# Samples' convolution taps as one GpSimd product and one VectorE sum, prompt taps in two chains, fewer taps on TensorE

## What is computed

```
def causal_dwconv(h, buf, w, b):          # h (B,T,C), buf (B,K-1,C), w (K,C), b (C)
    full = jnp.concatenate([buf.astype(h.dtype), h], axis=1)
    out = lax.conv_general_dilated(full, w[:, None, :], window_strides=(1,), padding="VALID", ...)
    return out + b.astype(h.dtype), full[:, full.shape[1] - (k - 1):]
...
proj = h @ p["w_in_ab"][i]
ya, pb = multi_scale_pool(xa, pool_bufs[i], start_pos, ...)
glu = a * jax.nn.sigmoid(gt)
c, cb = causal_dwconv(glu, conv_bufs[i], p["conv_w"][i], p["conv_b"][i])
yb = jax.nn.silu(layernorm(c, ...))
x = x + jnp.concatenate([ya, yb], axis=-1) @ p["w_out_ab"][i]
```

## Time and profile before

| | |
|---|---|
| median of 3 runs | 1206.99 us (1206.85 to 1207.07) |
| profiled execution | 1207.7 us, of which the traced span is 1205.9 us |
| PE, matmuls busy | 1186.9 us, 98% of the span |
| DVE / ACT / POOL busy | 741.7 / 508.6 / 623.7 us |
| stretch of units 3 to 11 and the convolution | from about 29 to 133 us of the span |

### The profile page before, as it was taken

How to read it: one execution, slowest core, us unless ns; L and a number is a source line. 1 busy time by engine, 2 the same in 40 slices (tenths; PEclk the granted TensorE clock), 3 DMA queues, 4 the chain that set the end, 5 groups by cost and what they waited for, 6 DMA issues and landing times.

```text
span 1205.9 us, 21702 instructions
## 1 busy us (share of the span) xinstructions
PE 1186.9 (98%) x8636; PEld 1156.7 (96%) x8636; DVE 741.7 (62%) x1499; ACT 508.6 (42%) x880; POOL 623.7 (52%) x632
## 2 busy tenths in 40 slices
PE   7999999999999999999999999999999999999997
PEld 7887799999999999999999999999999999999997
DVE  5999555567945688454521754345687557865554
ACT  6333455445434454343521532344443344433442
POOL 4643435436963469543455323443489344884433
PEclk9999999999999999999999999999999999999999
DMA  6310124321332213422322221322214222242212
GB/s 241 112 36 27 44 67 139 105 70 35 106 140 70 70 35 106 141 74 67 123 88 82 64 84 62 122 71 88 70 36 157 88 70 70 70 141 71 66 54 79
DMA packets 33652, 103.74 MB, mean 86 GB/s; under 512 B 4880, under 2 KB 6928, under 8 KB 33552
## 3 DMA queue, kind: packets, MB, share of 16 engines
q1 hardware_dynamic: 29488, 98.92, 25.0%
q10 hardware_dynamic: 4080, 3.69, 1.0%
HBM read 98.29 MB, written 4.79 MB: 85 GB/s over the span
## 4 chain that ended last, share of the span: by engine, by line
PE 89%; DVE 4%; ACT 2%; DMA 1%; issue 1%; POOL 1%; ACTq 0%; POOLq 0%; SPq 0%; DVEq 0%
PE psum L408 67%; PE psum L606 13%; PE psum L504 3%; PE psum L736 3%; DVE psum L1846 1%; DVE psum L1734 1%; PE psum L448 1%; POOL w_lo L1340 1%; DVE squares_sum L2002 1%; DMA w_raw<-in_w_down 1%; PE psum L686 1%; DVE block_lo L1734 1%; PE psum L456 0%; ACT psum L1061 0%; DVE arena L1971 0%
## 5 line engine op out<-in xcount | busy, mean ns | idle before, releaser
L408 PE MATMUL psum<-x_hi,w_hi 128*128 128x288 f32 x1856 | 402.0, 298 | 6.7 <-ACT w_hi L782 6.7
L408 PE MATMUL psum<-x_hi,w_lo 128*128 128x288 f32 x1856 | 398.6, 296 | 1.1 <-POOL w_lo L1260 1.1
L408 PE MATMUL psum<-x_lo,w_hi 128*128 128x288 f32 x1856 | 398.2, 296 | 0.0
L1260 POOL TENSOR_TENSOR w_lo<-w_raw,w_hi 128x1024 fp32r<-128x1024 f32 (+2 forms) x102 | 226.8, 2228 | 275.3 <-ACT w_hi L782 275.3
L408 PEld LDWEIGHTS psum<-x_hi,w_hi 128*128 128x128 f32 x1856 | 300.0, 189 | 8.8 <-ACT w_hi L782 6.6
L408 PEld LDWEIGHTS psum<-x_hi,w_lo 128*128 128x128 f32 x1856 | 299.9, 189 | 1.5 <-POOL w_lo L1260 1.5
L408 PEld LDWEIGHTS psum<-x_lo,w_hi 128*128 128x128 f32 x1856 | 300.0, 189 | 0.0
L1846 DVE SCALAR_TENSOR_TENSOR psum<-arena,params,psum 128x608 f32<-128x608 f32 x176 | 150.6, 856 | 88.5 <-ACT psum L1061 84.1
L1260 POOL TENSOR_TENSOR w_lo<-arena,w_hi 128x1024 fp32r<-128x1024 f32 (+1 forms) x49 | 114.6, 2338 | 119.9 <-ACT w_hi L782 119.9
L782 ACT ACTIVATE w_hi<-w_raw 128x1024 fp32r<-128x1024 f32 (+2 forms) x102 | 98.5, 970 | 88.5 <-PE psum L408 79.6
L606 PE MATMUL psum<-block_hi,w_hi 128*128 128x288 f32 x448 | 133.4, 298 | 0.2 <-POOL w_lo L1340 0.2
(11 more groups left out here) (208 smaller groups left out, 1619.2 us busy)
## 6 DMA issues: line engine op xcount, KB each, us to landing
w_raw<-in_w_up SPq DMA_DIRECT2D x44, 512.0 KB, 3.4
arena<-in_w_up SPq DMA_DIRECT2D x44, 512.0 KB, 3.4
w_raw<-in_w_down SPq DMA_DIRECT2D x16, 512.0 KB, 3.6
arena<-in_w_down SPq DMA_DIRECT2D x16, 512.0 KB, 3.6
w_raw<-in_w_in_c SPq DMA_DIRECT2D x16, 512.0 KB, 3.3
w_raw<-in_w_in_ab SPq DMA_DIRECT2D x12, 512.0 KB, 3.6
w_raw<-in_w_out_ab SPq DMA_DIRECT2D x16, 256.0 KB, 2.6
w_raw<-in_w_out_c SPq DMA_DIRECT2D x8, 512.0 KB, 3.4
```

Source lines behind the costliest of these rows:

```text
L408: last = nc.tensor.matmul(PS[:, 2 * (q % 2 if slot is None else slot) + half, 0:HALF], w[q][:, k * P:(k + 1) * P], r[:, r_at, half * HALF: ...
L1260: nc.gpsimd.tensor_tensor(w_lo[slot][:, 0:nk * P], raws[RAW_SLOT[RAW[u]]][:, 0:nk * P], w_hi[slot][:, 0:nk * P].bitcast(F32), ALU.subtract ...
```

## The change

The taps that PE does for the prompt are 6, 7, 7 and 10 for the four groups, and so DVE's are 25, 24, 24 and 21. DVE does them in two chains by even and odd taps, in the banks S1 and M1, and a new function `merge(c)` adds the two. For the samples POOL multiplies in one instruction (`sample_products`) each of 64 outputs' 31 inputs by the 31 tap weights, 1984 products for each partition, into a buffer `tap_products`; DVE sums over the taps with one `tensor_reduce` (`sum_samples`) and adds the bias with one `tensor_scalar` in `merge`. `sample_products(c)` for c > 0 waits until DVE has summed the group before, since there is one buffer. The chains "s" and "r" and `combine_samples` are gone.

```diff
-    PE_TAPS = 10
-    V_TAPS = TAPS - PE_TAPS
+    PE_TAPS = (6, 7, 7, 10)
+    V_TAPS = [TAPS - n for n in PE_TAPS]
...
-        tap_w = cut(XA0 + KH * XL + KH * GL, PE_TAPS, P)
+        tap_w = cut(XA0 + KH * XL + KH * GL, max(PE_TAPS), P)
+        tap_products = mem[:, (KD + KH) * T:(KD + KH) * T + SM * TAPS].rearrange("p (s t k) -> p s t k", s=NS, t=DS)
...
-                for n in range(PE_TAPS):
-                    k = V_TAPS + n
-                    pe.wait_ge(tap_w_ready, PE_TAPS * c + n + 1)
+                for n in range(PE_TAPS[c]):
+                    k = V_TAPS[c] + n
+                    pe.wait_ge(tap_w_ready, sum(PE_TAPS[:c]) + n + 1)
                     last = nc.tensor.matmul(PS[:, S0, 0:PR], tap_w[:, n, :], glu[:, c, k:k + PR],
-                                            start=(n == 0), stop=(n == PE_TAPS - 1))
+                                            start=(n == 0), stop=(n == PE_TAPS[c] - 1))
                 last.then_inc(conv_mm, 1)
...
-                for n in range(PE_TAPS):
+                for n in range(PE_TAPS[c]):
                     nc.scalar.activation(tap_w[:, n, :], ident[:, :], ACT.Copy,
-                                         scale=pcol("conv_w", (TAPS - PE_TAPS + n) * KH + c)).then_inc(tap_w_ready, 1)
+                                         scale=pcol("conv_w", (V_TAPS[c] + n) * KH + c)).then_inc(tap_w_ready, 1)
...
+            def sample_products(c):
+
+                pool.wait_ge(glu_ready, 2 * c + 2)
+                if c:
+                    pool.wait_ge(taps_summed, c)
+                else:
+                    pool.wait_ge(ld_par, 16)
+                first = glu[:, c, CB + PR:CB + PR + 1]
+                weights = pcol("conv_w", c)
+                nc.gpsimd.tensor_tensor(tap_products,
+                                        bass.AP(first.tensor, first.offset, [first.ap[0], [CB + DS, NS], [1, DS], [1, TAPS]]),
+                                        bass.AP(weights.tensor, weights.offset, [weights.ap[0], [0, NS], [0, DS], [KH, TAPS]]),
+                                        ALU.mult).then_inc(tap_products_ready, 1)
+
             for u in range(1, N_IN0):
                 split_n(u + 3)
+                if u in (2, 5, 8, 11):
+                    sample_products(u // 3)
                 if u in (3, 6, 9):
                     windows(u // 3 - 1)
...
-            steps_made = [0]
-
             def conv(c, first, end):
 
                 dve.wait_ge(glu_ready, 2 * c + 2)
-                if first == 0:
-                    behind.update(p=0, s=0, r=0)
-
-                def step(chain, out, k, acc, win, last=False):
-                    w = pcol("conv_w", k * KH + c)
-                    if behind[chain]:
-                        dve.wait_ge(conv_step, behind[chain])
-                        ins = nc.vector.scalar_tensor_tensor(out=out if last else acc, in0=win, scalar=w, in1=acc,
-                                                             op0=ALU.mult, op1=ALU.add)
-                    elif chain == "r":
+                if c and first == 0:
+                    dve.wait_ge(taps_merged, c)
+                for k in range(first, end):
+                    acc, win, w = PS[:, (S1, M1)[k % 2], 0:PR], glu[:, c, k:k + PR], pcol("conv_w", k * KH + c)
+                    if k == 0:
+                        ins = nc.vector.tensor_scalar(acc, win, w, pcol("conv_b", c), ALU.mult, ALU.add)
+                    elif k == 1:
                         ins = nc.vector.tensor_scalar(acc, win, w, None, ALU.mult)
                     else:
-                        ins = nc.vector.tensor_scalar(acc, win, w, pcol("conv_b", c), ALU.mult, ALU.add)
+                        dve.wait_ge(conv_step, sum(V_TAPS[:c]) + k - 1)
+                        ins = nc.vector.scalar_tensor_tensor(out=conv_o[:, c, 0:PR] if k == V_TAPS[c] - 1 else acc,
+                                                             in0=win, scalar=w, in1=acc, op0=ALU.mult, op1=ALU.add)
                     ins.then_inc(conv_step, 1)
-                    steps_made[0] += 1
-                    behind[chain] = steps_made[0]
-
-                new = smp(conv_o[:, c, PR:T])
-                samples = lambda k: smp(glu[:, c, CB + PR:GL], CB + DS)[:, :, k:k + DS]
-                for k in range(first, end):
-                    last = k == V_TAPS - 1
-                    step("p", conv_o[:, c, 0:PR], k, PS[:, S1, 0:PR], glu[:, c, k:k + PR], last)
-                    step("s", new, k, smp(PS[:, M1, 0:SM]), samples(k), last)
-                    if k % 2:
-                        step("r", None, V_TAPS + k // 2, smp(PS[:, M1, SM:2 * SM]), samples(V_TAPS + k // 2))
-
-            behind = dict(p=0, s=0, r=0)
-            CONV_STEPS = V_TAPS + TAPS
-            assert V_TAPS // 2 == PE_TAPS
+
+            def sum_samples(c):
+                dve.wait_ge(tap_products_ready, c + 1)
+                nc.vector.tensor_reduce(smp(conv_o[:, c, PR:T]), tap_products, AX.X, ALU.add).then_inc(taps_summed, 1)
+
+            def merge(c):
+
+                dve.wait_ge(conv_step, sum(V_TAPS[:c + 1]))
+                nc.vector.tensor_tensor(conv_o[:, c, 0:PR], PS[:, (S1, M1)[V_TAPS[c] % 2], 0:PR], conv_o[:, c, 0:PR],
+                                        ALU.add).then_inc(taps_merged, 1)
+                dve.wait_ge(taps_summed, c + 1)
+                nc.vector.tensor_scalar(conv_o[:, c, PR:T], conv_o[:, c, PR:T], pcol("conv_b", c), None, ALU.add)\
+                    .then_inc(conv_samples, 1)
 
             def combine(c):
 
                 dve.wait_ge(conv_mm, c + 1)
-                dve.wait_ge(conv_step, CONV_STEPS * (c + 1))
+                dve.wait_ge(taps_merged, c + 1)
                 nc.vector.tensor_tensor(conv_o[:, c, 0:PR], PS[:, S0, 0:PR], conv_o[:, c, 0:PR], ALU.add)\
                     .then_inc(conv_whole, 1)
-
-            def combine_samples(c):
-                dve.wait_ge(conv_step, CONV_STEPS * (c + 1))
-                nc.vector.tensor_tensor(conv_o[:, c, PR:T], PS[:, M1, SM:2 * SM], conv_o[:, c, PR:T], ALU.add)\
-                    .then_inc(conv_samples, 1)
...
@@ -1609,39 +1618,42 @@
             make_glu(0)
             conv(0, 0, 7)
             evacuate(3)
-            conv(0, 7, 14)
+            conv(0, 7, 15)
             evacuate(4)
-            conv(0, 14, V_TAPS)
             make_glu(1)
-            combine_samples(0)
-            conv(1, 0, 5)
+            conv(0, 15, V_TAPS[0])
+            sum_samples(0)
+            merge(0)
+            conv(1, 0, 2)
             combine(0)
-            conv(1, 5, 8)
             evacuate(5)
-            conv(1, 8, 14)
+            conv(1, 2, 10)
             evacuate(6)
-            conv(1, 14, 19)
+            conv(1, 10, 18)
             evacuate(7)
-            conv(1, 19, V_TAPS)
             make_glu(2)
-            combine_samples(1)
-            conv(2, 0, 5)
+            conv(1, 18, V_TAPS[1])
+            sum_samples(1)
+            merge(1)
+            conv(2, 0, 4)
             combine(1)
-            conv(2, 5, 9)
+            conv(2, 4, 6)
             evacuate(8)
-            conv(2, 9, 15)
+            conv(2, 6, 13)
             evacuate(9)
-            conv(2, 15, 20)
+            conv(2, 13, 20)
             evacuate(10)
-            conv(2, 20, V_TAPS)
             make_glu(3)
-            combine_samples(2)
-            conv(3, 0, 9)
+            conv(2, 20, V_TAPS[2])
+            sum_samples(2)
+            merge(2)
+            conv(3, 0, 3)
             combine(2)
-            conv(3, 9, 15)
+            conv(3, 3, 8)
             evacuate(11)
-            conv(3, 15, V_TAPS)
-            combine_samples(3)
+            conv(3, 8, V_TAPS[3])
+            sum_samples(3)
+            merge(3)
             combine(3)
```

More of the change, by code:

```diff
@@ L29 @@
 ACT = mybir.ActivationFunctionType
+AX = mybir.AxisListType
 P = 128
@@ L299, in hybrid_trunk @@
         conv_samples = sem("conv_samples")
+        tap_products_ready, taps_summed, taps_merged = sem("tap_products_ready"), sem("taps_summed"), sem("taps_merged")
         new_packed = sem("new_packed")
```

## The result

| | before | after |
|---|---|---|
| median of 6 runs each, us | 1207.19 (1206.85 to 1207.80) | 1212.54 (1211.11 to 1215.63) |
| profiled execution, time and span, us | 1207.7, 1205.9 | 1212.39, 1210.7 |
| start of `conv_mean` | 133.09 | 135.96 |
| length of `conv_mean` | 3.88 | 5.81 |

The ratio is 1.0046, with an interval of 1.0036 to 1.0056: slower by 0.46%. 1210.7 us was forecast, within 1204 to 1215.

What follows compares the result with a forecast made beforehand. PE was taken to bound the kernel, with DVE nearly as full. PE's saved 8.6 us would be lost to DVE's stalls of 13.35 and 3.3 us, `conv_mean` starting 3.7 us late: 1210.7 us, range 1204 to 1215.

Steps and rivals of the forecast that it cites:

- PE's part: Ten taps leave PE, 8.64 us; if nobody is late, `conv_mean` starts at 124.45 instead of 133.09.
- The forecast's 12 us of PE waiting for DVE: PE waits about 12 us for DVE, in pieces over units 7 and 10, the last taps and `conv_mean`.
- DVE's plain work: DVE's steps, merges, biases and sums without stalls: 24.1 us gone, 18.1 new, net 6.0 us less.
- POOL's product: Length T of POOL's one multiplication of 1984 columns: 4.9 us, between 3.6 and 5.5.
- rival C: A longer POOL product because weights are read four columns apart: 1212.5 us, or near 1215 or 1218; chance 0.15.
- The stalls at the bias: DVE's bias of groups 0, 1 and 2 waits for POOL's just-begun product: three times 4.45, 13.35 us.
- Rival A: No stall at DVE's bias, since so short or in-place an instruction passes POOL: 1198.4 us; chance 0.17.
- rival B: Fewer or shorter bias stalls: product 3.6 us, or POOL still at a low part for group 0; 1206.8 or 1206.2; chance 0.20.
- The glus: DVE's glus of groups 1 and 2 meet POOL's work: 2.7 and 0.6 us, together 3.3, between 0 and 6.
- The sum: All DVE terms added: `conv_mean` starts at 136.8 instead of 133.09, 3.7 us late.
- the branch of the forecast that had 0.48: Main case: POOL's product of 4.4 to 5.4 us, three bias stalls, 1209.2 to 1212.2 us; chance 0.48.
- Rival D, PE's clock: PE's clock restarting slower after gaps of a few us: hidden while PE waits for DVE, given nothing; no chance stated.

Runs made afterwards that it cites:

- first experiment: The changed kernel, but POOL's product of the next group waits for the bias of the group before instead of its sum; 1198.88 us, ratio 0.9935.
- The packed weights: The changed kernel, but ACT first copies each group's 31 tap weights side by side and POOL's product reads them there; 1210.14 us, ratio 1.0025.

## Why the prediction was right or wrong

**What bounds, and PE's part.** Right. PE's list got 8.6 us shorter, and `conv_mean` could have started near 124.5: with the stalls gone it starts at 124.64 (first experiment). The forecast's 12 us of PE waiting for DVE are there as 4.57 + 1.46 + 2.81 us of waits (for the 1.46 the view names no releaser; the wait ends at 119.03, 0.1 us behind DVE's combine of group 2, which these taps wait for) and some 2.4 us of matmuls at the lower clock between 93.9 and 99.4, whose pairs start 0.48 us apart there and 0.27 behind; together 11.2.

**DVE's plain work.** Right within 0.9 us. The sum takes 2.21 us where 2.13 and its end were taken from the additions, the tap steps keep 0.66 (eight from 60.34 on take 5.35 us, half of it beside POOL's product, eight from 66.27 on 5.34), and two chains cost nothing. DVE's last combine began at 135.18; less the stalls of 16.3 us that is 118.9, of which 0.37 is the wait for PE; the forecast had 119.4 without waits.

**POOL's product.** Mis-sized: T is 5.56 us, not 4.9, and just over the upper end of 5.5. I took the ns a column of the multiplications with few columns; 1984 columns go at (5.56 - 0.19) / 1984 = 2.71 ns, close to the slowest row. The packed weights, at 2.02 ns, show that a quarter of it is how the weights lie. The rule that rival C takes from the Trainium skill, "GPSIMD Engine Reference", section "Performance pitfalls for Q7 kernels" (half more cycles for a read step over 8 bytes), has the direction; on 4.19 us it would make 6.2, an estimate, and 5.56 was measured.

**The stalls at the bias.** The mechanism was right: the bias, 64 columns and in place, does wait, for the whole of POOL's instruction under way. Rival A fell. Two stalls of 4.98 us were there and not three of 4.45; the third escaped through rival B's mechanism (POOL still at its low parts), by 0.3 us, while the forecast had POOL free "by 1 us". POOL was free at 57.55, near the 57.1 of the forecast, but DVE's sum was over at 56.65 and not at 58.4, mostly because group 1's glu had lost 1.2 us and not 2.7. Group 3's bias, forecast to meet none, met a low part and lost 0.83. With 0.18 at group 0 that is 10.97 us in all against 13.35.

**The glus.** Mis-sized the other way: 5.3 us against 3.3. The one of group 2 was given 0.6 us and lost 3.5, for each of its two instructions waited for a low part of 2.4 us. Group 1's lost 1.2 where 2.7 were set, and group 3's, set at nothing, 0.6. The forecast's range for the glus, 0 to 6, held it.

**The sum.** 136.8 was forecast for `conv_mean`, 135.96 came: -0.5 of plain work and DVE's one wait, -2.4 of biases, +2.0 of glus. Part of the agreement is luck: errors of 2.4 and 2.0 us cancel. The 1212.54 us stand just above the branch of the forecast that had 0.48 (three stalls, 1209.2 to 1212.2) and on rival C's 1212.5, but C's three stalls of 5.05 us were not there: two stalls and the clock made the number, and its agreement with C is chance.

**Rival D, PE's clock.** This is the step that failed. "A slower restart would be hidden: behind the last taps PE has some 6 us until DVE is ready. I give it nothing." It is hidden after the gap before 93.93, as said. But the last gap stands directly ahead of `conv_mean`, where nothing of DVE's lateness is left to hide behind, and there it cost 1.93 us. Of these 1.7 are the clock, since `conv_mean` takes 4.12 us at full clock behind a wait (first experiment), and 0.2 come with any wait (3.88 without one). With the 1.93 the forecast would have been 1212.6 us against 1212.54 measured; that this fits to 0.1 us is luck again, for `conv_mean` started 0.8 us earlier than forecast, and the runs spread over 4.5 us.

The Trainium skill, "SBUF — State Buffer", section "Who interferes with whom", calls the pair of ports to SBUF that VectorE shares with GpSimd an exclusive lock, held for a whole instruction by whoever comes first. The traces agree: the bias takes 5.2 us beside a product of 5.5, 1.2 beside a piece of 1.5, 0.24 with nothing beside it. Group 0's, which came before a low part had ended, took 0.40 and went ahead of the product that was next. It holds the other way too: of the two low parts beside group 2's glu the first took 2.35 us and the second, which the glu's first instruction had gone ahead of, 2.79. The same section has `tensor_reduce` never contend on trn2; the sum takes 2.20 us at 54.52, wholly beside POOL's low parts, and 2.21 at 80.47, beside nothing.

## What to carry to other kernels

Look at what an instruction's semaphore releases: here the sum released a POOL instruction of 5.5 us 0.4 us ahead of a DVE instruction that needs what POOL then holds, and a release one instruction later was worth some 13 us (from a ratio of 1.0046 to 0.9935). Where two engines share something, give the short user its turn first, or cut the long one into pieces. Do not add stalls up as if each stood alone: one that appears early can move the engine past a later one, as group 0's bias did for group 2's glu. And price a wait of PE not by its length alone: where work of PE that sets the end stands directly behind it, add what the lower clock takes.

## What the runs showed that I had not expected

- PE's granted clock fell after some gaps and not after others. Right behind waits of 2.41, 2.81 and 4.57 us the pieces of 4 us read between 0.54 and 0.89; after 0.65, 1.31 and 1.56 us nothing of it is to be seen in the profiles (`conv_mean` in 4.12 us behind the waits of 0.65 and 1.56). But three of the six runs with the product in four pieces, whose profile has waits of 1.45 and 1.56 us, had a lower mean clock than the profiled one and took 2 to 4 us more: a wait that costs no clock in one run may do so in another. Those three have no profile, so this is not shown. The piece from 132 to 136 us of the change, most of it a wait, still reads 1.00. The Trainium skill, "TensorE: Matmul & The Clock Gate", "Part 1: The HAM clock gate", has the same two levels, with activity as what gives the higher one; the traces agree.
- A product on POOL in which one operand's elements lie 16 bytes apart took 2.71 ns a column, with them side by side 2.02.
- A faster POOL instruction can make a DVE stall appear where there was none: with the shorter product, group 0's bias went from 0.40 to 3.91 us.
